# Attentions of a three-block network: maps and heads in pairs, values as the stationary operand

## The reference, cut to what matters

```python
# diff: 4 heads of 128 = 2 maps of 64
logits = einsum('bqhmd,bkhmd->bhmqk', qi, k) * scale      # causal
p = softmax(logits);  p = p[:, :, 0] - lam * p[:, :, 1]
oa = rms_norm(p @ v, diff_sub_g) * (1 - lam_init)
# fox: 8 heads of 64
logits = q @ k.T * scale + (c_i - c_k)                    # causal, decayed
ob = softmax(logits) @ v
x = x + rms_norm(concat(oa, ob) @ w_out, attn_post_g)
```

## Time and profile before

| | us |
|---|---|
| three runs, median (lowest to highest) | 2400.82 (2399.33 to 2405.96) |
| the profiled execution | 2408.14 |
| its span on the core | 2406.8 |
| TensorE matmul busy | 2290.1 |
| VectorE, ScalarE, GpSimd busy | 1051.9, 828.3, 62.9 |
| mean granted clock of TensorE | 0.971 |

### The profile page before, as it was taken

The page is one execution under the profiler, slowest core; times in us unless marked ns, Lnnn a source line. Parts: engine busy times, 40 slices in busy tenths (PEclk is TensorE's granted clock), DMA queues, the critical chain, the costliest instruction groups (busy, mean ns, idle before and its releaser), DMA issues.

```text
span 2406.8 us, 26573 instructions
## 1 busy us (share of the span) xinstructions
PE 2290.1 (95%) x10796; PEld 1829.2 (76%) x10796; DVE 1051.9 (44%) x2179; ACT 828.3 (34%) x1618; POOL 62.9 (3%) x87
## 2 busy tenths in 40 slices
PE   6899999999998999899999989888999999999998
PEld 5667678888887767688888878777666688888886
DVE  6264454323335454453333356544555544333333
ACT  4144343323224353342222243332333433322232
POOL 3000000000000000000000000000000000000000
PEclk9899999999999999999999999989788899999999
DMA  6511123323332212123333223215111032333331
GB/s 151 115 47 53 40 70 105 96 90 104 96 94 70 79 45 63 47 82 95 99 100 94 95 66 107 65 48 114 29 29 31 23 106 87 101 97 99 94 100 66
DMA packets 273600, 192.17 MB, mean 80 GB/s; under 512 B 21933, under 2 KB 241237, under 8 KB 273477
## 3 DMA queue, kind: packets, MB, share of 16 engines
q1 hardware_dynamic: 268576, 177.76, 25.6%
q0 software_dynamic: 4752, 12.67, 2.3%
q10 hardware_dynamic: 148, 0.04, 0.0%
HBM read 186.21 MB, written 4.23 MB: 79 GB/s over the span
## 4 chain that ended last, share of the span: by engine, by line
PE 84%; ACT 6%; DVE 6%; DMA 2%; issue 2%; POOL 0%; DVEq 0%; ACTq 0%; POOLq 0%
PE bank L513 52%; PE bank L553 7%; PE bank L555 7%; PE bank L554 7%; PE bank L591 3%; PE bank L589 3%; PE bank L599 2%; DMA weights<-in_w_in_dram 2%; ACT token_scratch L1504 1%; ACT h_features L1511 1%; PE bank L592 1%; ACT arena L1546 1%; ACT weights_hi_lo L1483 1%; DVE weights_hi_lo L839 1%; DVE arena L871 0%
## 5 line engine op out<-in xcount | busy, mean ns | idle before, releaser
L513 PE MATMUL bank<-h_features,weights_hi_lo 128*128 128x512 f32 (+1 forms) x5160 | 1140.3, 382 | 15.6 <-DVE weights_hi_lo L839 7.9
L513 PEld LDWEIGHTS bank<-h_features,weights_hi_lo 128*128 128x128 f32 x5160 | 935.7, 190 | 206.0 <-issue 17.0
L839 DVE TENSOR_TENSOR weights_hi_lo<-weights,weights_hi_lo 128x1024 fp32r<-128x1024 f32 (+1 forms) x337 | 399.4, 1189 | 690.2 <-ACT weights_hi_lo L1483 689.7
L1483 ACT ACTIVATE weights_hi_lo<-weights 128x1024 fp32r<-128x1024 f32 (+1 forms) x337 | 340.9, 1016 | 393.5 <-PE bank L555 344.8
L554 PE MATMUL bank<-weights_hi_lo,hidden 128*128 128x512 f32 x528 | 205.4, 389 | 0.0
L553 PE MATMUL bank<-weights_hi_lo,hidden 128*128 128x512 f32 x528 | 205.4, 389 | 0.0
L555 PE MATMUL bank<-weights_hi_lo,hidden 128*128 128x512 f32 x528 | 205.4, 389 | 0.0
L513 PE MATMUL bank<-arena 128*128 128x128 f32 (+4 forms) x864 | 143.6, 296 | 13.3 <-ACT arena L1561 11.7
L1546 ACT ACTIVATE arena<-arena,row_stats 128x128 f32<-128x128 f32 (+3 forms) x160 | 81.5, 510 | 188.4 <-DVE row_stats L941 188.4
L1608 ACT ACTIVATE hidden<-arena 128x512 fp32r<-128x512 f32 x66 | 41.7, 632 | 300.0 <-DVE arena L1030 300.0
L513 PEld LDWEIGHTS bank<-arena 128*128 128x128 f32 (+4 forms) x864 | 120.4, 204 | 26.7 <-ACT arena L1561 18.0
(11 more groups left out here) (312 smaller groups left out, 1943.6 us busy)
## 6 DMA issues: line engine op xcount, KB each, us to landing
weights<-in_w_in_dram SPq DMA_DIRECT2D x84, 512.0 KB, 3.9
weights<-in_w_gate_dram SPq DMA_DIRECT2D x66, 512.0 KB, 3.8
weights<-in_w_up_dram SPq DMA_DIRECT2D x66, 512.0 KB, 3.8
weights<-in_w_down_dram SPq DMA_DIRECT2D x60, 512.0 KB, 3.7
weights<-in_w_out_dram SPq DMA_DIRECT2D x24, 512.0 KB, 3.6
bias_rows<-decay_scratch POOLq DMA_DIRECT2D x16, 256.0 KB, 3.5
weights<-in_w_branch_dram SPq DMA_DIRECT2D x16, 256.0 KB, 2.8
weights<-in_w_cmp_dram SPq DMA_DIRECT2D x16, 256.0 KB, 4.4
```

Of the source, the lines that this page charges most:

```text
L513: last = e.matmul(out_ap, l, r, start=(j == 0), stop=(j == len(pairs) - 1))
L839: e.tensor_tensor(pair_view(i, 1), raw_view(i), pair_view(i, 0).bitcast(F32), ALU.subtract).then_inc(done, tick(("split", i)))
L1483: e.activation(pair_view(i, 0), raw_view(i), ACT.Copy).then_inc(done, tick(("hi", i)))
```

## The change

Steps take the place of units (`Step`). A step holds one tile t of 128 queries for two maps (diff), two fox heads 2m and 2m + 1, or two NSA heads rr and rr + 4: 32 steps in a layer, 48 in NSA, where a pair's four compressed steps are followed by four selected and four window steps. The two lie on partitions 0 to 63 and 64 to 127 of queries and keys.

```diff
 def scores(u):
+    outs = [bank((*u.name, "s", j)) for j in range(2)]
     for j, (l, r) in enumerate(u.maps):
-        out_ap = bank((*u.name, "s", j))
-        if u.kind == "nsa":
-            e.matmul(out_ap[:, 0:u.w], l, r, start=True, stop=True).then_inc(...)
-        else:
-            e.matmul(out_ap[:, 0:u.w], l, r, start=True, stop=False)
-            e.matmul(out_ap[:, u.w - P:u.w], IDB[:, :], MKB[:, :], start=False, stop=True)
+        last = e.matmul(outs[j][:, 0:u.w], l, r, start=True, stop=u.kind == "nsa")
+        if u.kind == "nsa":
+            last.then_inc(done, tick((*u.name, "s", j)))
+    if u.kind != "nsa":
+        for j, out_ap in enumerate(outs):
+            e.matmul(out_ap[:, u.w - P:u.w], IDB[:, :], MKB[:, :], start=False, stop=True)
```

```diff
-        matmuls(out_ap[:, 0:P], [(weights[0:n, c:c + P], u.values[c // P]) for c, n in CHUNKS(u)])
+    def weigh_values(g):
...
+        for r, c0, c1, l, moving, start, stop in g.products:
+            last = e.matmul(out_ap[r, c0:c1], l, moving, start=start, stop=stop)
...
+                        for j, r in enumerate(halves):
+                            at = 512 + m * P + HD * j
+                            products.append((r, c0, 256, V[:, kt, at:at + HD], ATTN_P[hf][:, j, kt, c0:256], kt == 0, kt == t))
```

As queries are columns of the result, the reciprocals and gates can't be applied behind the product any more. GpSimd scales the rows ahead of the transposes, and the transposes wait for it:

```diff
+    def attend(s, rows, bias_of, fill):      # GpSimd
...
+            if u.kind != "diff":
+                pool.wait_ge(dve.done, dve[*u.name, "norm"])
+                for j in range(2):
+                    row = rows[(2 * (i - 1) + j) % 6][:, 0:u.w]
+                    e.tensor_scalar(row, row, st[:, 6 + j:7 + j], None, ALU.mult)
```

```diff
-                    attend(UNITS[s], ATTN_E, ATTN_P, ready, fill)
-                    pe.wait_ge(dve.done, dve[s, "heads"])
-                    turn_rows(s, TOK, ND)
+                    attend(s, ATTN_E, ready, fill)
```

More of the change, by code:

```diff
@@ L444, in program @@
-        UNITS = {f"L{layer}": layer_units(f"L{layer}") for layer in range(LAYERS)}
-        UNITS["M"] = nsa_units()
-        CHUNKS = lambda u: [(c, min(P, u.w - c)) for c in range(0, u.w, P)]
+        @dataclass
+        class Group:
+            name: tuple
+            steps: list
+            products: list
+            bank: tuple
+            width: int
+            first: bool
+            final: bool
+            tile: int
+            half: int
+        CHUNKS = lambda u: [(c, min(P, u.w - c)) for c in range(0, u.w, P)]
@@ L487, in emit, with row_free, turned_by_vector @@
             sp = Lane(sync, None, None)
-            banks, turns = Ring(PSUM, known(4)), Ring(TURN, known(5))
+            banks = Ring(PSUM, known(4), {None: list(range(8)), "step": list(range(7)), "values": [7]})
+            turns = Ring(TURN, known(5))
+            def row_free(old, j):
+                if old.kind == "diff" and j == 1:
+                    return dve.done, dve[*old.name, "mixed"]
+                return pe.done, pe[*old.name, "turned", j]
+            def turned_by_vector(u, j):
+                return u.t % 2 == 0 if u.kind == "diff" else j == 0
             def tensor_program():
@@ new lines, in weigh_values @@
+                def weigh_values(g):
+                    if g.first:
+                        out_ap = bank(g.bank, "values")
+                    else:
+                        out_ap = banks[g.bank]
+                    for u in g.steps:
+                        for j in range(len(u.turned)):
+                            lane = dve if turned_by_vector(u, j) else act
+                            pe.wait_ge(lane.done, lane[*u.name, "pt", j])
+                    for r, c0, c1, l, moving, start, stop in g.products:
+                        last = e.matmul(out_ap[r, c0:c1], l, moving, start=start, stop=stop)
+                    last.then_inc(done, tick(g.name))
@@ L912, in attend @@
[L912 to L928 removed]
+                def attend(s, rows, fill):
+                    steps, groups = STEPS[s]
+                    n = len(steps)
+                    row = lambda i, j: rows[(2 * i + j) % 6]
+                    for i in range(n + LAG):
```

575 lines of the change are left out of this document (297 added, 278 removed).

## The result

The changed kernel takes **2300.93 us** (median of four runs, 2297.79 to 2303.38) against 2403.39 (2399.33 to 2415.25) for the kernel before beside it: ratio 0.9563, 95% interval 0.9539 to 0.9587. Forecast were 2302 and a range of 2270 to 2362. The profiled execution took 2303.38 us. One of the five executions of the first experiment took 3553.66 us at a mean granted clock of 0.557, and no reading rests on it.

The account below looks back on a forecast made before the run. TensorE's queue was taken as the bound, hardly waiting. Two layers at -28 us each (-56) and NSA at -43 made -99 from the median of 2400.8: 2302 us, range 2270 to 2362.

Parts of the forecast that it names:

- 9.4: Scores in pairs: fewer entries and fixed costs on TensorE save 9.4 us per layer.
- 3.4: Diff heads' normalisation in the fox steps: ones-matmuls on TensorE for four heads add 3.4 us per layer.
- the 28: Sum of the terms for one layer's attention: 28 us saved, including 2 us of added waits.
- Streams of a pair: Two scores on separate row halves overlap, three slots for four instructions: -8.5 us per layer and in NSA.
- The rival of halves in turn: Array halves never work at once, so streams and values save nothing: 2350 us in all, chance 0.30.
- Values side by side: Two heads' value products overlap on different array columns: -6.5 us per layer, -13.7 in NSA.
- Scaling on GpSimd: Rows scaled before the transposes, two instructions per fox or NSA step: 0.7 us each at 512, upper end 1.28.
- the 15 at which I called myself wrong: Sign against the prediction: transposes wait for GpSimd more than 15 us in all.
- the second rival: Halves overlap, but the chain through other engines becomes the bound in NSA: about 2325 us, chance 0.15.
- The end: End of a layer's attention: turned tiles and waits go, squares and the last chain are added, net -9 us per layer.
- NSA: NSA attention falls from 233.5 to 190 us, -43, with the mean clock kept at 0.84.
- the slower rival: Half the array may not hold the clock; layers' fox and diff steps drop to the lower level: 2450 us, chance 0.06.

Follow-up runs that it names:

- the first experiment: The scaling of fox and NSA rows moved from GpSimd to VectorE, against the changed kernel; 2271.35 us, ratio 0.9432.
- e6: Scaling on VectorE and both scores of a step on partitions 0 to 63, against the kernel with scaling on VectorE; 2326.01 us.
- e7: Scaling on VectorE and each value group's products sorted head by head, against the kernel with scaling on VectorE; 2291.27 us.
- e5: The scaling moved from GpSimd to VectorE against the changed kernel, run again for its profile; 2271.58 us, ratio 0.9443.
- e4: Value products sorted head by head, scaling still on GpSimd, against the changed kernel; 2307.40 us, ratio 0.9587.
- e11: VectorE's splits of a diff head and first w_out weights put behind the step's copies, against the kernel with scaling on VectorE; 2273.91 us.
- e10: The ones-matmul of the diff heads' squares made twice, against the kernel with scaling on VectorE; 2283.35 us, ratio 0.9475.

## Why the prediction was right, and where it was not

**The bound.** TensorE's queue was it, as read: over the three stretches its busy time fell by 138.9 us, its idle time rose by 32.2, and 106.7 came off. In the first layer busy time fell by 35.3 us, where my terms had 9.4 + 8.5 + 6.5 + 6.6 (turns) - 3.4 = 27.6; idle time rose by 6.4, where the rest of the 28, waits added and taken, had it fall by 0.4. The errors, 7.7 and 6.8, nearly cancel, and 28.9 stands beside 28. That the total is met so closely is luck.

**Streams of a pair** (-8.5 per stretch) was mis-sized by half, and its premise failed: I took three slots of four, because matmuls start in the order of the queue and the two of one score need the same half. In the trace four instructions fill two slots. Two start at 189.465 and 189.471, the other two at 189.999 and 190.005. On one half no two start together (282.912, 283.446, 283.875 and 284.304 in e6), so each of these pairs is one instruction of either score. The removal of the pairing cost 54.4 us, clock included; three of four would have been 25. Of the rule that the Trainium skill ("TensorE: Matmul & The Clock Gate", Packing small matmuls — row/col tiling) gives, the side-by-side part is borne out, at 6 ns between the starts. That they start in order is not: the sorted value products of e7 show starts of the second head ahead of the first head's last, at 271.787 and 271.896, and the measurement decides. The rival of halves in turn is out: it had a 512 step at 1.71 us.

**Values side by side** (-6.5, -6.5, -13.7) was right in kind: 1.66 us for sixteen, which start in eight pairs (six of 256 columns, 0.215 apart, two of 128, 0.11 apart), where I had one slot of 0.21 more. Undone by order alone it costs 5.9, 7.4 and 9.4 in the stretches.

**Scaling on GpSimd** is the step that failed. I took 0.7 us with 1.28 as the upper end, on the reasoning that one input less comes to about half. It takes 1.61, and the transposes wait 24.5 us for it, over the 15 at which I called myself wrong; 14.3 of these are in NSA and 5.8 and 4.4 in the layers. The price of a wait failed too. I put 10 us more of waits into NSA, 12 at its clock of 0.84; taking the long scaling away gave NSA 24.7 us, 18.2 of it through a higher clock. So the second rival, the chain, came true in part, beside an overlap larger than either case had. One figure was met by luck: NSA's transposes wait 14.3 us for GpSimd, beside the 14 that my sum made of scalings of 0.7. The Trainium skill ("GPSIMD Engine Reference", Engine selection and Performance versus the Vector engine) puts one-input work near line rate, by my estimate from it 0.44 us; the trace does not agree, and here the form with two tensors is even the faster, 1.13.

**The end** (-9) came to -1.6 and -1.8. The turns went, 6.6 and their wait of 2.8, but 12.6 us stand in place of 14.2, because I gave the last rounds' chain 2 to 3 us. The chain of the last two steps there is 6.2 us of GpSimd alone. With VectorE it is 8.9, with the bank emptied first 8.5. The output matmul did come 3.2 us behind the start of the last value products, but by the lower clock; in the second layer and in e5 it is 1.66.

**NSA** (-43) came to -49.4, with the mean clock at the 0.84 that I had kept; the streams' second half is in it, and idle time rose by 20.5 where I had 10 at full clock. That both held is partly luck: the kernels without GpSimd's long scaling show 0.88 to 0.93 there with the same matmuls, and e4, which keeps it, shows 0.92.

**The clock in the layers** did not fall as a whole (0.98, from 0.98 and 0.99), so the slower rival is out. **VectorE** was busy for half of NSA, far from 75%.

## What to carry to other kernels

In these runs small fp32 matmuls of contraction 64, or with 64 stationary columns, ran fully beside their partner where it stood next in the list; lay the products out in turn, and reckon with half the streams. Before a stage goes to GpSimd in series with TensorE, find a row of that very form, and put a range above the nearest row as well as below it. And reckon a wait of TensorE at more than its length where a stretch runs at both clock levels, as NSA does here: 45 us of waits cost 76. How much more is uncertain, because the clock of such a stretch differs between kernels with the same waits (0.84 and 0.92).

## What the runs showed of the hardware that was not expected

- GpSimd's product with a factor per partition took 1607 ns at 128 x 512, 1278 at 384, 922 at 256 and 730 at 128; the product of two tensors with the factor broadcast 1133, 828, 614 and 403; VectorE's form with a factor 484, 418, 350 and 284.
- The NSA stretch of e5 and e11 has the same instructions, and lasted 161.1 us at a mean clock of 0.93 and 166.0 at 0.90, with the same idle time (19.6 and 19.7); in e10, also with the same instructions, 166.1 at 0.90. A difference of 5 us between two kernels is therefore not yet one of their code; the ones-matmul may be such a case, with 11.8 us for 6.9.
- Leaving one half of the rows idle in the scores (e6 against e5) lowered the clock of the layers from 0.99 and 1.00 to 0.96, with TensorE busy for a larger share of the time, 95% in place of 92.
- Two value products on different halves of the columns started out of the order of the list in e7: two of the second head's, 256 columns wide, ahead of the first head's last two, 128 wide.
